# Sliding-window attention of a two-layer trunk: masked bias rows, sinks read in place, one sum per head pair, projections in halves

## The reference

```python
    q, k, v = _split(h @ w_in + b_in, B_SIZES)
    kk, vv = with_prev(k), with_prev(v)
    logits = jnp.einsum('bnqkgd,bnskd->bnkgqs', q, kk) * (Dh ** -0.5)
    rel = (W + jnp.arange(W))[:, None] - jnp.arange(2 * W)[None, :]
    in_win = (rel >= 0) & (rel < W)
    bias = rel_bias[rel_bucket(rel)]
    logits = jnp.where(mask, logits + bias, -jnp.inf)
    p = jax.nn.softmax(jnp.concatenate([logits, sink], axis=-1), axis=-1)[..., :-1]
    o = jnp.einsum('bnkgqs,bnskd->bnqkgd', p, vv)
    return o.reshape(B, T, N_HEADS * Dh) @ w_out + b_out
```

## Time and profile before

| | before |
|---|---|
| median of 3 runs | 1240.52 us |
| the profiled execution, its own time | 1238.56 us |
| its span, first to last instruction | 1236.8 us |
| TensorE busy | 1174.0 us (95%) |
| VectorE (DVE) busy | 639.0 us (52%) |
| ScalarE (ACT) busy | 467.1 us (38%) |
| GpSimd (POOL) busy | 573.2 us (46%) |
| mean granted TensorE clock | 0.987 of full speed |

### The profile page before, as it was taken

How to read it: one execution, slowest core, us unless ns; L and a number is a source line. 1 busy time by engine, 2 the same in 40 slices (tenths; PEclk the granted TensorE clock), 3 DMA queues, 4 the chain that set the end, 5 groups by cost and what they waited for, 6 DMA issues and landing times.

```text
span 1236.8 us, 16936 instructions
## 1 busy us (share of the span) xinstructions
PE 1174.0 (95%) x5580; PEld 963.5 (78%) x5580; DVE 639.0 (52%) x1095; ACT 467.1 (38%) x872; POOL 573.2 (46%) x336
## 2 busy tenths in 40 slices
PE   5999988889999999999999989799999999999996
PEld 4768876678788888888888778778888888888885
DVE  5479889994554444443222369955544444431111
ACT  4252156664333322223222367734322333222222
POOL 4335486654445544454444554314345554444441
PEclk8999999999999999999999999899999999999998
DMA  5722311103333333322333342203333333323331
GB/s 160 248 78 68 121 37 39 40 19 103 103 87 86 100 102 102 102 80 71 93 93 104 103 123 55 64 1 103 103 101 88 84 99 102 91 70 94 93 93 68
DMA packets 178709, 110.37 MB, mean 89 GB/s; under 512 B 7425, under 2 KB 173372, under 8 KB 178668
## 3 DMA queue, kind: packets, MB, share of 16 engines
q1 hardware_dynamic: 178224, 108.69, 30.9%
q10 hardware_dynamic: 444, 1.16, 0.3%
HBM read 107.70 MB, written 6.33 MB: 92 GB/s over the span
## 4 chain that ended last, share of the span: by engine, by line
PE 80%; DVE 10%; issue 4%; DMA 2%; POOL 2%; ACT 1%; SPq 0%; DVEq 0%; ACTq 0%; POOLq 0%
PE ps L608 26%; PE ps L610 25%; PE ps L609 25%; DVE prob L1557 1%; POOL w_lo L480 1%; PE ps L792 1%; DVE raw L1557 1%; DMA b_toep<-bias_toep 1%; DMA q_all<-in_x 1%; DVE prob L1579 1%; DVE work L1506 1%; DVE b_prob L1752 1%; DVE ss L1447 1%; PE ps L617 1%; DVE raw L1579 1%
## 5 line engine op out<-in xcount | busy, mean ns | idle before, releaser
L480 POOL TENSOR_TENSOR w_lo<-raw,w_hi 128x1024 fp32r<-128x1024 f32 (+1 forms) x200 | 462.9, 2336 | 546.0 <-ACT w_hi L1043 545.8
L608 PE MATMUL ps<-xs_hi,w_hi 128*128 128x512 f32 x960 | 379.2, 395 | 5.2 <-DVE x L1430 3.4
L609 PE MATMUL ps<-xs_lo,w_hi 128*128 128x512 f32 x960 | 374.6, 390 | 0.0
L610 PE MATMUL ps<-xs_hi,w_lo 128*128 128x512 f32 x960 | 374.5, 390 | 0.0
L1043 ACT CAST w_hi<-raw 128x1024 fp32r<-128x1024 f32 (+1 forms) x200 | 183.0, 964 | 469.5 <-PE ps L610 457.2
L608 PEld LDWEIGHTS ps<-xs_hi,w_hi 128*128 128x128 f32 x960 | 180.7, 188 | 48.3 <-DVE x L1430 3.7
L609 PEld LDWEIGHTS ps<-xs_lo,w_hi 128*128 128x128 f32 x960 | 180.8, 188 | 38.0 <-issue 1.2
L610 PEld LDWEIGHTS ps<-xs_hi,w_lo 128*128 128x128 f32 x960 | 180.8, 188 | 38.0
L608 PE MATMUL ps<-act_hi,w_hi 128*128 128x512 f32 x352 | 139.2, 396 | 0.0
L610 PE MATMUL ps<-act_hi,w_lo 128*128 128x512 f32 x352 | 138.0, 392 | 0.0
L609 PE MATMUL ps<-act_lo,w_hi 128*128 128x512 f32 x352 | 136.6, 388 | 0.0
(11 more groups left out here) (191 smaller groups left out, 1511.8 us busy)
## 6 DMA issues: line engine op xcount, KB each, us to landing
raw<-in_ffn_w_gate_up SPq DMA_DIRECT2D x88, 512.0 KB, 4.9
raw<-in_ffn_w_down SPq DMA_DIRECT2D x32, 384.0 KB, 3.6
raw<-in_a_w_in SPq DMA_DIRECT2D x21, 512.0 KB, 4.7
raw<-in_ffn_w_down SPq DMA_DIRECT2D x32, 320.0 KB, 4.0
raw<-in_b_w_in SPq DMA_DIRECT2D x10, 512.0 KB, 5.2
bias_toep<-bias_row SPq DMA_DIRECT2D x1, 4096.0 KB, 18.4
toep<-bias_toep SPq DMA_DIRECT2D x16, 256.0 KB, 2.6
raw<-in_a_w_out SPq DMA_DIRECT2D x8, 512.0 KB, 4.1
```

Source lines behind the costliest of these rows:

```text
L480: nc.gpsimd.tensor_tensor(pieces(w_lo, n)[half], pieces(raw, n)[half], pieces(w_hi, n)[half].bitcast(F32), ALU.subtract)\
L608: nc.tensor.matmul(dst, wh, xh, start=start, stop=False, **kw)
L609: nc.tensor.matmul(dst, wh, xl, start=False, stop=False, **kw)
L610: return nc.tensor.matmul(dst, wl, xh, start=False, stop=stop, **kw)
```

## The change

It has six parts.

1. The bias row of each head gets a second part of 384 values for attention B, in which distances outside the window already carry the mask value (a 33rd row of the one-hot table, against a row of ones that DVE writes: `rel_one`). `hot` is 33 x 1024 instead of 32 x 640, the second matmul and DVE's second copy are 512 wide instead of 128, and the mask `window` (256 columns of `tab`) is gone.
2. Once attention A has read its bias, SP issues a second skewed copy (16 x 128 x 256, 2 MB) into the first 256 columns of `bias_toep`, ahead of the slabs of the first feed-forward block.
3. POOL's sixteen additions of the window are gone, with `b_bm`; DVE reads `b_toep`. SP's loads of pair j >= 2 wait for DVE's reductions of pair j - 2 (`bneg_done`) instead of POOL's additions.
4. The sink copies are gone; DVE and ACT read one column of `nsink` and `sink` in place.
5. Sum and reciprocal are made once per pair over 8 columns (`b_invert`), at the start of DVE's next step, which waits for ACT's exponentials of both heads. The eight scalings (`b_normalise`) stay on DVE, after the second low part.
6. Projections are cut into halves of 12 matmuls: `FORE` (k = 0 to 3) and `REAR` (k = 4 to 7). Units 5, 6 and 7 start one step earlier: step 2 has the first half of unit 5, step 3 the second half of 5 and the first of 6, step 4 the second of 6 and the first of 7, step 5 the second of 7. `b_scale` of units 5, 6 and 7 stays in steps 3, 4 and 5.

```diff
+FORE, REAR = range(0, DM // 2), range(DM // 2, DM)
+Q_PARTS = {0: ((3, FORE), (3, REAR)), 1: ((4, FORE), (4, REAR)), 2: ((5, FORE),), 3: ((5, REAR), (6, FORE)),
+           4: ((6, REAR), (7, FORE)), 5: ((7, REAR),)}
...
+    t[BUCKETS, C_HOT + ROW_A:] = np.where((place >= T) | (place < T - P), BIG, 0)[ROW_A:]
...
+            sp.wait_ge(neg_done, 4 * H)
+            skew_b = bass.AP(tensor=bias_row.tensor, offset=ROW_A + P - 1, ap=[[GLEN, H], [-1, P], [1, 2 * P]])
+            sp.dma_start(bias_toep[:, :, 0:2 * P], skew_b).then_inc(toep_out, 16)
...
-                        sp.wait_ge(bbias_done, 2 * (j - 1))
-                    sp.dma_start(b_toep[:, par, a, :], bias_toep[j + a * (H // 2), :, T - 2 * P:T])\
+                        sp.wait_ge(bneg_done, 8 * (j - 1))
+                    sp.dma_start(b_toep[:, par, a, :], bias_toep[j + a * (H // 2), :, 0:2 * P])\
...
-                    nc.gpsimd.tensor_tensor(b_bm[:, par, a, :], b_toep[:, par, a, :], window, ALU.add)\
-                        .then_inc(bbias_done, 1)
...
-            def b_project(u):
+            def b_project(u, ks=range(DM)):
...
-                pe.wait_ge(bqr_done, u)
-                pe.wait_ge(lo_done, 2 * n + 2)
-                for k in range(DM):
+                if ks[0] == 0:
+                    pe.wait_ge(bqr_done, u)
+                    pe.wait_ge(lo_done, 2 * n + 2)
+                for k in ks:
...
-                if k in Q_OF_STEP:
-                    b_project(Q_OF_STEP[k])
+                for u, ks in Q_PARTS.get(k, ()):
+                    b_project(u, ks)
...
+            def b_invert(k):
+                par = k % 2
+                sums = b_rsum[:, par, :, :].rearrange("p a i -> p (a i)")
+                dve.wait_ge(bsinkp_done, 2 * k + 2)
+                nc.vector.tensor_tensor(sums, sums, b_sinkp[:, par, :, :].rearrange("p a i -> p (a i)"), ALU.add)\
+                    .then_inc(brs_done, 1)
+                dve.wait_ge(brs_done, k + 1)
+                nc.vector.reciprocal(b_rinv[:, par, :, :].rearrange("p a i -> p (a i)"), sums).then_inc(brinv_done, 1)
...
-                        for two, one in ((sink2, sink), (nsink2, nsink)):
-                            nc.vector.tensor_copy(two[:, par, a:a + 1], one[:, bass.ds(j, 1)])\
-                                .then_inc(bsink2_done, 1)
...
+                if 1 <= k < DM + 1:
+                    b_invert(k - 1)
                 if 2 <= k < DM + 2:
                     lo_heads(0)
...
+                if 1 <= k < DM + 1:
+                    for a in range(2):
+                        b_normalise(k - 1, a)
                 if k in Q_OF_STEP:
                     b_scale(Q_OF_STEP[k])
```

More of the change, by code:

```diff
@@ L55 @@
 WIN = 7 * P
-C_ID, C_DUP, C_CAUSAL, C_WIN, C_HOT = 0, P, 2 * P, 3 * P, 5 * P
-GLEN = 640
+C_ID, C_DUP, C_CAUSAL, C_HOT = 0, P, 2 * P, 3 * P
+ROW_A, ROW_B = 640, 384
+GLEN = ROW_A + ROW_B
 C_END = C_HOT + GLEN
@@ L105, in tables @@
     t[:, C_CAUSAL:C_CAUSAL + P] = np.where(i[None, :] <= i[:, None], 0, BIG)
-    rel = P + i[:, None] - np.arange(2 * P)[None, :]
-    t[:, C_WIN:C_WIN + 2 * P] = np.where((rel >= 0) & (rel < P), 0, BIG)
-    dist = np.maximum(T - 1 - np.arange(GLEN), 0)
+    place = np.concatenate([np.arange(ROW_A), np.arange(ROW_A - ROW_B, ROW_A)])
+    dist = np.maximum(T - 1 - place, 0)
     exact = BUCKETS // 2
@@ L179, in trunk @@
         x_tok = q_all[:, 0:DM, :].rearrange("p a b -> p (a b)").rearrange("p (t n) -> p t n", t=NB)
-        hot = q_all[0:BUCKETS, 8:10, :].rearrange("p a b -> p (a b)")[:, 0:GLEN]
-        rel_sb = q_all[0:BUCKETS, 10, 0:H]
+        hot = q_all[0:BUCKETS + 1, 8:10, :].rearrange("p a b -> p (a b)")[:, 0:GLEN]
+        rel_sb = q_all[0:BUCKETS + 1, 10, 0:H]
         g_sb = q_all[0:H, 11:13, :].rearrange("p a b -> p (a b)")[:, 0:GLEN]
@@ L240, in trunk @@
         causal = tab[:, C_CAUSAL:C_CAUSAL + P]
-        window = tab[:, C_WIN:C_WIN + 2 * P]
         G_ATTN, G_FFN, G_FINAL, B_IN, B_OUT, G_LAT = (0, 8), (16, 24), 32, 40, 50, 58
@@ L292, in trunk @@
         btoep_full = [sem("btoep_full0"), sem("btoep_full1")]
[L293 to L296, removed]
+        bqh_done, bql_done, blg_done, bneg_done = (sem(n) for n in ("bqh_done", "bql_done", "blg_done", "bneg_done"))
+        bsinkp_done, brs_done, brinv_done = sem("bsinkp_done"), sem("brs_done"), sem("brinv_done")
+        bnrm_done = [sem("bnrm_done0"), sem("bnrm_done1")]
         bpt_done, bpth_done, bptl_done, bo_done, boh_done, bol_done = (
@@ L582, in _ @@
             for j in range(DM):
-                par = j % 2
                 pool.wait_ge(bqh_done, j + 1)
[L586 to L593, removed]
-                    nc.gpsimd.tensor_tensor(b_bm[:, par, a, :], b_toep[:, par, a, :], window, ALU.add)\
-                        .then_inc(bbias_done, 1)
+                nc.gpsimd.tensor_tensor(bq_lo[:, j % 2, :], bq_raw[:, j % 2, :],
+                                        bq_hi[:, j % 2, :].bitcast(F32), ALU.subtract).then_inc(bql_done, 1)
                 if j in (0, 2, 5, 7):
@@ L934, in b_project @@
                                xh(k), xl(k), k == 0, k == DM - 1)
-                last.then_inc(unit_done, 1)
+                if ks[-1] == DM - 1:
+                    last.then_inc(unit_done, 1)
             def b_turn(h2, a, k):
@@ L1084, in _ @@
                     act.dma_start(par_rows, par_in).then_inc(small_in, 16)
-            act.dma_start(hot, consts[0:BUCKETS, C_HOT:C_END]).then_inc(hot_in, 16)
-            act.dma_start(rel_sb, rel_bias).then_inc(hot_in, 16)
+            act.dma_start(hot, consts[0:BUCKETS + 1, C_HOT:C_END]).then_inc(hot_in, 16)
+            act.dma_start(rel_sb[0:BUCKETS, :], rel_bias).then_inc(hot_in, 16)
             act.wait_ge(set_up, 4)
@@ L1360, in b_step @@
                                                  accum_out=b_rsum[:, par, a, i:i + 1])
+                        j = k + a * (H // 2)
                         nc.scalar.activation(b_sinkp[:, par, a, :], b_low[:, par, a, :], ACT.Exp,
-                                             bias=sink2[:, par, a:a + 1]).then_inc(bsinkp_done, 1)
+                                             bias=sink[:, j:j + 1]).then_inc(bsinkp_done, 1)
                 if 2 <= k < DM + 2:
@@ L1691, in _, with b_normalise @@
             b_scale(2)
+            def b_invert(k):
[6 more added lines that the diff above has]
+                nc.vector.reciprocal(b_rinv[:, par, :, :].rearrange("p a i -> p (a i)"), sums).then_inc(brinv_done, 1)
+            def b_normalise(k, a):
+                dve.wait_ge(brinv_done, k + 1)
+                for i in range(NB):
+                    n = P if i == 0 else 2 * P
+                    at = b_prob[:, k % 2, a, OFFB[i]:OFFB[i] + n]
+                    nc.vector.tensor_scalar(at, at, b_rinv[:, k % 2, a, i:i + 1], None, ALU.mult)\
+                        .then_inc(bnrm_done[a], 1)
             def b_step(k):
                 par = k % 2
[L1695 to L1702, removed]
-                        for two, one in ((sink2, sink), (nsink2, nsink)):
-                            nc.vector.tensor_copy(two[:, par, a:a + 1], one[:, bass.ds(j, 1)])\
-                                .then_inc(bsink2_done, 1)
+                if k == 0:
+                    dve.wait_ge(sink_done, 1)
                 def lo_heads(a):
```

33 lines of the change are left out of this document (10 added, 23 removed).

## The result

The changed kernel took 1247.41 us in the median of 14 runs (1242.56 to 1251.64), the kernel before 1240.26 us on the same chip (1238.22 to 1242.45). The ratio is 1.0061 with a 95% interval of 1.005 to 1.0072: slower by 7 us, where +4.5 us were forecast. The profiled execution took 1247.14 us, its span 1245.4 us against 1236.8; it lies 0.3 us under its median, that of the kernel before 1.7 us under its own, so a difference read from the two traces (8.6 us) is 1.4 us larger than that of the medians.

A forecast was written before the change was run, and what follows sets the result against it. TensorE, busy for 95% of the span, was taken as the bound; +0.6 us at full clock and +3.9 for low clock made +4.5 on 1238.56, 1243.1; with the median 2.0 above, 1245.0 us, range 1238.5 to 1249.5.

The forecast's parts named there:

- The bound and the place: Attention B, steps 3 and 4: TensorE idles about 3.5 and 6 us before a projection half, released by DVE's copy.
- Step 1, -4.2 us: Attention B: without window additions POOL's slab part ends sooner, so step 2 starts at 737.05 instead of 741.25 us.
- Steps 2, 5 and 6: Attention B: 8.7, 8.7 and 10.8 us long, changes of -0.2, -2.9 and -0.9 us.
- Steps 3 and 4 at full clock: Attention B: DVE and TensorE in series, 15.1 us against 11.5 (+3.6) and 17.9 against 12.4 (+5.4).
- The clock, +3.9 us: Attention B: TensorE runs at its low clock behind the two new waits, costing 1.6 and 2.3 us.
- The second copy and the wider table, 0 us: Upstream of attention B: second copy lands in 9 to 18 us, taken as 0 (to +1); table changes 0.
- The sum: Whole kernel: +0.6 us at full clock and +3.9 for the low clock, +4.5 us in all.
- The clock holds: Rival, steps 3 and 4: low clock falls into the idle times, not behind them; +0.6, 1241.1 us; chance 0.22.
- The wait does not bind: Rival, step 3: DVE copies unit 5 early enough, no serial loop; -9.3, 1231.2 us; chance 0.12 including small terms.
- DVE wins the pair: Rival, steps 4 and 6: all eight scalings pass before POOL's second half; 4.2 us less, 1240.8 us; chance 0.06.
- More is late: Rival, attention B: low clock also covers values and next logits, 5.5 us, with further delays; 1249 us; chance 0.10.

The follow-up runs named there:

- e5_fill: The changed kernel with 14 and 26 extra matmuls filling TensorE's waits in steps 3 and 4: 1242.83 us, ratio 1.0037 to the kernel before.
- e1_whole: The changed kernel with part 6 undone, units 5 to 7 projected whole: 1236.56 us, ratio 0.9981 to the kernel before.
- e8_split_copy: The changed kernel with whole projections and the second skewed copy in four later pieces: 1234.45 us, ratio 0.9962 to the kernel before.
- e9_before_pitch: The kernel before with rows of bias_row 1024 values apart instead of 640: 1242.12 us, ratio 1.0022 to the kernel before.
- e11_change_pitch: The changed kernel, halves included, with rows of bias_row 1088 values apart instead of 1024: 1245.54 us, ratio 1.0049 to the kernel before.
- e2_copy_first: The changed kernel with DVE copying the projected unit before the eight scalings in steps 3 to 5: 1236.83 us, ratio 0.9985.
- e6_both: The changed kernel with DVE's copy before the scalings and TensorE's values before the next half projection: 1236.51 us, ratio 0.9979.

## Why the prediction was right, and where it was not

- **The bound and the place.** Right. The loss stands at the first `xs_hi, w_hi` matmul in steps 3 and 4, released by `bq_raw`; the waits are 3.25 and 5.91 us, 3.5 and 6.2 forecast.
- **Step 1, -4.2 us.** Right. Step 2 starts at 737.56, forecast 737.05; from the first reduction of step 0 it is 14.62 us, forecast 14.67. The slab part runs from 730.41 instead of 729.65, and the scalings take 3.92 us beside it.
- **Steps 2, 5 and 6.** 8.9, 8.8 and 10.6 us; forecast 8.7, 8.7 and 10.8.
- **Steps 3 and 4 at full clock.** 15.1 and 17.8 in `e5_fill`, forecast 15.1 and 17.9. The parts were read right: one scaling got between POOL's two instructions, the others waited.
- **The clock, +3.9 us.** The mechanism held, the size was short. It cost 2.6 us in each of steps 3 and 4, forecast 1.6 and 2.3, because TensorE was low over the whole half projection behind the first wait as well (5.5 us from its start on). The 1.6 came from a row in which the low clock ended sooner after a shorter idle time; the row at the start, behind 3.39 us of idle time, was the nearer one for 3.25 us. A further 1.0 us fell in step 7 (10.2 us; 9.1 before, 9.2 in `e5_fill`), whose logits ran low behind the idle times of step 6 (TensorE is busy for 6.7 of its 10.6 us); no term stood for it. It isn't the halves' doing, since `e1_whole` has it too, and `e8_split_copy`, with the same steps, has not: why it comes in one execution and not in another stays open. The window of the changed kernel there:

```profile
804.00:808.00 4.00, 4.00 (x31) 3.78 (x31) 3.04 (x13) 0.52 (x3) 0.00 (x0) 0.51 1.10 238
```

  With it the measured sum is 6.2 us, without it 5.2.
- **The second copy and the wider table, 0 us.** This step failed. I scaled the copy by size from the row of 18.4 us and allowed 9 to 18; it took 22.1, and I did not look at what the change does to the first copy at all: 24.7 us. The bound of +1 was for the second alone, and it held: POOL's slab parts from 295 to 343 us take 48.4 us, 0.5 more than before. The first had no term. `e9_before_pitch` puts it at 3.0 us, `e11_change_pitch` puts both at 1.9. In the profiled execution upstream is only 0.6 us later than before, the least of the eight kernels with that pitch.
- **The sum.** Attention B came out at +7.7 us against +4.5: 2.3 of the 3.2 us are the clock (6.2 instead of 3.9), and 0.9 is full-clock time, +1.5 instead of +0.6. Of this 0.9, 0.6 stands behind step 7: from the start of step 8 to the last `bo_lo` it is 19.0 us, 18.4 before, and so in every kernel with parts 1 to 5. The prediction had nothing there; no run shows which part it is. The forecast of 1245.0 lay 2.4 under the median. That it lay no further off is partly luck: 3.2 us missing in attention B and 1.9 for the pitch would be 5.1, and the medians differ by 2.7 more than forecast. Upstream differs by that much between kernels whose instructions there are the same.
- **The rivals.** *The clock holds* is out by the windows and `e5_fill`. *The wait does not bind* named the right point: with the copy earlier (`e2_copy_first`) attention B is within 0.8 us of that with whole projections (1.3 us in steps 2 to 6), and the kernel is faster than before. Its price was too low. It had -9.3 us, and `e6_both`, where TensorE hardly waits for the copy, has -6.2 in attention B: step 4 takes 13.5 us and step 5 9.6, where 11.5 and 8.7 were reckoned. *DVE wins the pair* is out, 4.74 us for the eight scalings. *More is late* is nearest in size, by its clock of 5.5 us, but not in its mechanism: the low level ended with the half projection (0.98 granted from 760 to 764 us) and did not reach over the values and the next logits.

## What to carry to other kernels

Cutting a job in halves so that it starts earlier pays only if what frees its buffer comes earlier too. Before splitting, look at where the release stands in the other engine's step: if it is last, the two engines fall in series. A new wait can also bring the low clock: behind waits of 3.25 and 5.91 us the half projection took 5.3 us instead of 2.8, behind one of 1.25 us (`e2_copy_first`) 2.85. And when a table in memory grows, look at the distance of its rows as well as at its size: here the copy that nobody had touched became a third slower.

## What was not expected of the hardware

A skewed copy from memory to memory (rows of 2048 bytes, each read 4 bytes further left) took 18.4 and 19.3 us with source rows 2560 bytes apart, 19.2 to 20.8 with 4352, and 24.7 to 25.9 with 4096. For the copy of half the size it was 14.2 to 14.8 with 4352 and 21.7 to 22.4 with 4096. The cost of such a copy isn't in proportion to its bytes: half the bytes in the same number of rows took about three quarters of the time at 4352, and 0.85 to 0.89 of it at 4096. Why 4096 is slow no run here shows. The Trainium skill ("DMA: Bandwidth & Descriptors", Latency and other measured facts) tells of slow copies at row distances of large powers of two and advises padding; its cases are of 512 KiB and more, and 192 bytes of padding did not help there. Here 256 bytes of padding on 4096 were enough.
